# A decoder layer on one core: the shift of the normalized rows moves from an accumulating DMA to an add on GpSimd

## What is computed

```python
    merged = jax.nn.sigmoid(gate_a) * (o_a @ w_branch_a) + jax.nn.sigmoid(gate_b) * (o_g @ w_branch_b)
    x = x + gate1 * (merged @ w_out)
    h2 = rms_norm(x, norm2_g) * (1 + scale2) + shift2
    x = x + gate2 * hier_moe(h2, ...)      # top-2 of 32 experts, each w_gate, w_up (1024 x 512), w_down (512 x 1024)
```

## Time and profile before

| | us |
|---|---|
| median of 3 runs (lowest, highest) | 1292.85 (1291.79, 1295.52) |
| the profiled execution, its own time | 1294.05 |
| its span in the profile | 1292.1 |
| row stage and routing, until the first gather is issued | about 720 to 796 |
| experts | about 802 to 1290 |
| PE busy, DVE busy, ACT busy, POOL busy | 1159.8, 523.0, 224.9, 230.0 |

### The profile page before, as it was taken

The page is one execution under the profiler, slowest core; times in us unless marked ns, Lnnn a source line. Parts: engine busy times, 40 slices in busy tenths (PEclk is TensorE's granted clock), DMA queues, the critical chain, the costliest instruction groups (busy, mean ns, idle before and its releaser), DMA issues.

```text
span 1292.1 us, 20453 instructions
## 1 busy us (share of the span) xinstructions
PE 1159.8 (90%) x7849; PEld 731.6 (57%) x7849; DVE 523.0 (40%) x1094; ACT 224.9 (17%) x506; POOL 230.0 (18%) x279
## 2 busy tenths in 40 slices
PE   4999998999999999999999997999978788778796
PEld 2344443475667668888887455656544354444463
DVE  3398967534253454454454447221211111111112
ACT  4122225331222321101100222000000000000000
POOL 2432344200010411520000001111111101111000
PEclk9999999999999999999999996999999989999999
DMA  9998999998243444224434727999999999999994
GB/s 355 371 287 281 356 378 384 377 386 307 92 142 128 127 118 103 58 64 113 122 131 146 261 65 246 421 416 414 413 420 418 418 415 420 416 414 418 414 414 168
DMA packets 118392, 368.15 MB, mean 285 GB/s; under 512 B 12604, under 2 KB 58573, under 8 KB 98966
## 3 DMA queue, kind: packets, MB, share of 16 engines
q1 hardware_dynamic: 93408, 304.44, 60.8%
q0 software_dynamic: 21328, 55.24, 13.9%
q10 hardware_dynamic: 3558, 7.13, 1.8%
HBM read 354.61 MB, written 22.36 MB: 292 GB/s over the span
## 4 chain that ended last, share of the span: by engine, by line
PE 63%; DMA 24%; SPq 4%; DVE 4%; issue 3%; ACT 2%; ACTq 0%; DVEq 0%; POOLq 0%
PE ps L1941 60%; DMA hx<-in_w_exp_gate 10%; DMA ring<-in_w_exp_gate 6%; DMA ring<-in_w_exp_up 4%; PE ps L1952 3%; SPq L583 2%; DMA ring<-in_cache_v 1%; DMA ring<-in_cache_k 1%; SPq L588 1%; DMA work<-in_x_prompt 1%; DMA h_rows<-ring 1%; SPq L556 1%; DVE work L1896 0%; SPq L554 0%; DVE ring L1316 0%
## 5 line engine op out<-in xcount | busy, mean ns | idle before, releaser
L1941 PE MATMUL ps<-ring,work 128*64 128x256 f32 (+4 forms) x2064 | 294.0, 436 | 42.5 <-DMA ring<-in_w_exp_up 17.0
L1941 PEld LDWEIGHTS ps<-ring,work 128*64 128x64 f32 (+2 forms) x2064 | 156.1, 138 | 162.4 <-issue 83.2
L1941 PE MATMUL ps<-hx,ring 128*128 128x272 f32 x928 | 215.0, 393 | 4.1 <-DVE work L1560 4.1
L1941 PE MATMUL ps<-ring,hx 128*32 128x256 f32 (+3 forms) x1232 | 209.4, 463 | 8.5 <-ACT hx L879 4.2
L1941 PEld LDWEIGHTS ps<-hx,ring 128*128 128x128 f32 x928 | 175.7, 190 | 41.3 <-issue 4.2
L1941 PEld LDWEIGHTS ps<-ring,hx 128*32 128x32 f32 (+1 forms) x1232 | 108.1, 139 | 95.2 <-issue 76.4
L1941 PE MATMUL ps<-work 128*32 128x256 f32 (+12 forms) x1186 | 133.7, 397 | 20.8 <-DVE work L1255 10.0
L1941 PE MATMUL ps<-hx,work 128*64 128x256 f32 (+2 forms) x784 | 113.9, 411 | 22.8 <-DMA hx<-in_w_exp_up 9.0
L1894 DVE TENSOR_TENSOR work<-work,ps 128x256 f32<-128x256 f32 x32 | 13.5, 421 | 251.0 <-ACT work L1200 251.0
L800 POOL DMA_INDIRECT out<-work x32 | 50.5, 1578 | 327.8 <-DVE work L1906 327.8
L1941 PEld LDWEIGHTS ps<-hx,work 128*64 128x64 f32 (+2 forms) x784 | 69.5, 144 | 67.3 <-issue 30.9
(11 more groups left out here) (333 smaller groups left out, 931.0 us busy)
## 6 DMA issues: line engine op xcount, KB each, us to landing
ring<-in_w_exp_gate SPq DMA_DIRECT2D x21, 2048.0 KB, 40.8
ring<-in_w_exp_down SPq DMA_DIRECT2D x42, 1024.0 KB, 39.1
ring<-in_w_exp_up SPq DMA_DIRECT2D x21, 2048.0 KB, 40.4
ring<-in_w_ada SPq DMA_DIRECT2D x12, 2048.0 KB, 17.2
hx<-in_w_exp_gate SPq DMA_DIRECT2D x11, 2048.0 KB, 41.1
hx<-in_w_exp_up SPq DMA_DIRECT2D x10, 2048.0 KB, 38.9
work<-in_w_exp_down SPq DMA_DIRECT2D x20, 1024.0 KB, 39.3
ring<-in_cache_v SPq DMA_DIRECT2D x64, 256.0 KB, 9.6
```

The lines of the kernel that those rows point to most:

```text
L1941: return pe.matmul(out, lhsT, rhs, start=start, stop=stop, **k)
```

## The change

1. **The shift on GpSimd.** ACT's early fill of `h2_dram` is gone. The shift lies in a new tile `row_c` (in slot 5): sample shifts are loaded by ACT beside the other sample rows, the prompt's by SP (`shift_in`) after step 0's store. POOL adds `row_c` in place to each scaled tile, one TENSOR_TENSOR of 128 x 1024 for each step (32 x 1024 for step 0), and counts `h2_full`.
2. **Plain stores.** SP stores each tile to `h2_dram` (`rows_out`), at fixed places in its program: step 0 first, steps 1 and 2 behind the residual stores of steps 2 and 3, step 3 behind the load of expert 2's up, step 4 behind the load of expert 1's gate and the last residual store.
3. **Turned rows in `mergedT`.** `h2T[n]` is now that step's own columns in `mergedT`, five places in place of two, so ACT's copy no longer waits for the router's product (`lg_ps`). `out_part` takes the place of `h2g[1]`.
4. **First gate product.** For expert 0, TensorE starts the gate product on the first half of `xsT` and waits for the second half before k = 4.

```diff
-        h2T = [grid(ring[:, 5, D * (i + 2):D * (i + 3)], KD) for i in range(2)]
-        out_part = grid(ring[:, 5, 3 * D:4 * D], 2)
+        h2T = [mergedT[:, :, TILES[a][0]:TILES[a][0] + TILES[a][1]] for a in LATE]
+        out_part = grid(h2g[1], 2)
+        row_c = ring[:, 5, 2 * D:3 * D]
...
+            def rows_out(n):
+                t0, T = TILES[LATE[n]]
+                sp.wait_ge(s("h2_full"), n + 1)
+                sp.dma_start(h2_dram[t0:t0 + T, :], h2g[n % 2][0:T, :]).then_inc(s(f"h2_out{n % 2}"), 16)
+
+            rows_out(0)
+            sp.dma_start(row_c, bass.AP(tensor=mod_dram.tensor, offset=0, ap=[[0, P], [1, D]])).then_inc(s("shift_in"), 16)
             for n in range(1, PT):
                 residual_out(n)
+                if n > 1:
+                    rows_out(n - 1)
             sp.wait_ge(*stream[BEFORE_EXPERTS[4]][2])
             gate_up_load(2, 1, expert_row(2))
+            rows_out(PT - 1)
             sp.wait_ge(s("out_ps"), 2 * PT + 2)
             gate_up_load(1, 0, expert_row(1))
             residual_out(PT)
+            rows_out(PT)
...
                 pool.wait_ge(s("h2_rows"), n + 1)
-                pool.dma_start(h2_dram[t0:t0 + T, :], h2g[n % 2][0:T, :], accum_op=ALU.add).then_inc(s(f"h2_out{n % 2}"), 16)
+                if n == 0:
+                    pool.wait_ge(s("late_in"), 16 * 3)
+                elif n == 1:
+                    pool.wait_ge(s("shift_in"), 16)
+                v = h2g[n % 2][0:T, :]
+                pool.tensor_tensor(v, v, row_c[0:T, :], ALU.add).then_inc(s("h2_full"), 1)
...
-                if u == 0:
-                    act.wait_ge(s("late_out"), 64)
-                    act.dma_start(h2_dram[0:SEQ, :], late_source(0, 0, [0, SEQ])).then_inc(s("late_in"), 16)
-                    act.dma_start(h2_dram[SEQ:, :], late_source(0, 1, [D, DEC_B], [0, DEC_T])).then_inc(s("late_in"), 16)
...
-            late_rows_in(2, 3, 1, [D, DEC_B], [0, DEC_T])
+            act.wait_ge(s("late_out"), 64)
+            for v, kind in ((row_a, 2), (row_b, 3), (row_c, 0)):
+                act.dma_start(v[0:NS, :], late_source(kind, 1, [D, DEC_B], [0, DEC_T])).then_inc(s("late_in"), 16)
...
-                if n >= 2:
-                    act.wait_ge(s("lg_ps"), n - 1)
-                act.activation(h2T[n % 2][:, 4 * q:4 * q + 4, 0:T], grid(ps[:, 4 + q, 0:4 * T], 4), ACT.Copy).then_inc(s("h2T"), 1)
+                act.activation(h2T[n][:, 4 * q:4 * q + 4, :], grid(ps[:, 4 + q, 0:4 * T], 4), ACT.Copy).then_inc(s("h2T"), 1)
...
-                    dve.wait_ge(s("late_in"), 16 * (4 if n == 0 else 6))
+                    dve.wait_ge(s("late_in"), 16 * (3 if n == 0 else 5))
...
-                pe.wait_ge(s("xsT"), n)
+                ahead = isinstance(e, int) and e == 0
+                pe.wait_ge(s("xsT"), n - 1 if ahead else n)
...
+                        if ahead and m == 0 and k == KD // 2:
+                            pe.wait_ge(s("xsT"), n)
```

More of the change, by code:

```diff
@@ L1109, in _ @@
                 first_taken(OUT_GATE, u)
-                if u == 0:
-                    act.wait_ge(s("late_out"), 64)
-                    act.dma_start(h2_dram[0:SEQ, :], late_source(0, 0, [0, SEQ])).then_inc(s("late_in"), 16)
-                    act.dma_start(h2_dram[SEQ:, :], late_source(0, 1, [D, DEC_B], [0, DEC_T])).then_inc(s("late_in"), 16)
-                elif u == 1:
+                if u == 1:
                     act.wait_ge(s("state_p_out"), 16 * GH)
-                else:
+                elif u > 1:
                     act.wait_ge(s("o_gated"), u - 1)
@@ L1170, in _ @@
                     act.wait_ge(s("h2_gained"), 2)
-                    late_rows_in(2, 3, 0, [0, P])
+                    for v, kind in ((row_a, 2), (row_b, 3)):
+                        act.dma_start(v, late_source(kind, 0, [0, P])).then_inc(s("late_in"), 16)
                 turned_taken(n, 0)
@@ L1907, in dve_step @@
                 dve.tensor_scalar(weighted[par], ps[:, 4 + par, :], weight, None, ALU.mult).then_inc(s("weighted"), 1)
-            dve.wait_ge(s("late_in"), 16 * 16)
+            dve.wait_ge(s("late_in"), 16 * 15)
             for e in range(NE):
@@ L2517, in logits_of @@
                 for k in ks:
-                    last = mm(ps[0:T, 6, m * a:m * a + m], h2T[n % 2][:, k, 0:T], wr[:, k, 0:m], k == 0, k == KD - 1, skip_group_check=True)
+                    last = mm(ps[0:T, 6, m * a:m * a + m], h2T[n][:, k, :], wr[:, k, 0:m], k == 0, k == KD - 1, skip_group_check=True)
                 if ks[-1] == KD - 1:
```

## The result

| us | before | after |
|---|---|---|
| median (lowest, highest), 7 runs each | 1293.37 (1291.79, 1295.52) | 1298.04 (1296.08, 1300.18) |
| the profiled execution, its own time | 1294.05 | 1296.08 |
| its span | 1292.1 | 1294.1 |
| SP issues the residual rows' load: end of the merge, **M** | 707.33 | 705.04 |
| DVE starts the last tile's scaling (step 4, half 1), **S** | 781.23 | 783.61 |

The account below looks back on a forecast made before the run. The expert weight stream bounds the kernel, its start held by the gathers. A gather 0.66 us sooner, less 0.15 for ACT's loads, left 0.5 us; from the 1292.85 median the forecast was 1292.3 us, range 1290.1 to 1294.4.

Parts of the forecast that it names:

- the earlier tiles: Steps 0 to 3, before the last tile: POOL's adds run into DVE, nobody on the path late; without cover, up to 0.5 us a tile.
- What bounds the kernel: Expert phase: the weight stream keeps the DMA engines full, so the end is the stream's start, at 801.87 us, plus a constant.
- The add, the collision, the index: Last tile: POOL's 2.35 us add holds up a DVE add, moving the index 1.68 us to 794.17; forecast case, 62%.
- The plain store: Last tile's row store in SP's queue behind gate load and residual store: lands at 791.5, before the index.
- my case of slow values: Last store: residual lands after 9.8 us as before, at 792.5, and the rows at 793.8 to 795.1; slower-store rival 12%.
- What travels with it: ACT's ten small expert loads move nearer the first gather; cost to the gathers 0 to 0.5 us, taken as 0.15.
- my rivals: Besides the forecast: index not delayed 17%, store late 12%, collisions at steps 1 to 3 reach TensorE 5%, stream not following gathers 4%.
- the tail's terms: Last tile to expert 1's down load: add, store, index, gather 0.66 us sooner, ACT's small loads 0.15; leaves 0.5 us gain.

## Why the prediction was wrong

I forecast 1292.3 us (1290.1 to 1294.4), a gain of 0.5, with 93% on no difference. It became 1298.04, a loss of 4.7 us. The step that failed is the one on the earlier tiles, ahead of the part that I worked out.

- **What bounds the kernel**: right. The stream of weights decides, and its start and the end moved together (2.36 us for down, 2.0 for the span, between the profiles).
- **The add, the collision, the index**: right. The add was forecast at 2.35 us and took it, from S + 4.60 (forecast 4.69). DVE's instruction was stretched to 1.38 us, where I had said 1.8, because it came 1.0 us into the add and not 0.5: the ranking began 0.38 us later, since TensorE's eight small products ahead of it took 1.48 us in place of 1.08, and the add hid that. The index was forecast at 794.17, S + 12.94, and was ready at S + 12.85. The gather was forecast at S + 13.83 and came at 13.81, released by DVE. The Trainium skill (SBUF — State Buffer, "SBUF: two separate sides") says that the two take a shared pair of ports exclusively, for a whole instruction. The trace agrees: 0.16 us became 0.92 to 1.76 in the seven profiles with the add (how much depends on when it comes during it), and stayed 0.16 in the one without.
- **The plain store**: the value was too good. I took 791.5, S + 10.3, on the ground that gate and residual would land after 7.5 us without the accumulate beside them. They took 9.9 and 9.7, about as before, and the store landed near S + 12.4, close to my case of slow values (S + 12.6 and later). Two readings behind it were wrong. The accumulate had not slowed the two loads ahead, and it had not overtaken them: they had landed by 790.7 and 792.5, it landed at 794.83, and POOL's queue moved 0.02 of its 0.5 MB before 790 us. That the error cost nothing is luck: the index was later still, by 0.5 us.
- **What travels with it**: the term was mis-sized. I put the shift of ACT's ten loads at 0.15 us (0 to 0.5); the stretch from gather to down grew by 0.66, and the variant with early loads gives 0.9 back. It took the whole gain of the gather.
- **The earlier tiles**: this is where the sum failed. I looked at the collisions of POOL's adds (they cost nothing: 50.55 us from step 1 to S with and without them) and costed the load of the *prompt's* shift. The load of the *sample* rows' shift, which the same item of the change adds as the third of ACT's small loads, and DVE's wait for all three at step 0 (`late_in` 3), got no term at all. The rows needed were in the trace of before: DVE's step 0 with its idle time ended by TensorE, SP's 6 MB issued just ahead of ACT's loads, and the small loads' last packets at 717, some 2.3 us before they were needed. A third load of the same size behind them had to be asked for its landing. It came 2.99 us after the time at which DVE had begun before.
- **The clock**: no case of mine had TensorE run dry in the row stage and pay for it a second time. The 2.99 us of wait became 4.67.

The range was built from the tail's terms and from the spread of the runs; none of my rivals had a place ahead of step 1, so the one mechanism that decided was outside all of them. The tail came out close to even (0.02 us from S to down), so the sum missed the half microsecond there too, by the ten loads. What isn't settled is the share of the DMA engines that a small load gets beside another queue's megabytes, and why the store of the variant without the last add took 9.6 us.

## What to carry to other kernels

A small load that is added to a group under one semaphore makes every waiter of that group wait for the last of them: give each use its own count, or let only the engine that reads the data wait for it. Price it by what else is queued at that moment in the other queues, not by its bytes, and look at how much time the waiter's present releaser leaves. When an engine that feeds TensorE is made to wait on the path, add to the wait what TensorE's lower clock costs behind it, and ask which reused buffer hands the delay on.

## What the runs showed of the hardware

- A load of 128 KB took 12.05 us behind 6 MB that another queue had just been given, and at most 6.25 when 4 of the 6 were held back. Holding them back moved the loss to ACT's next load, of 1 MB.
- A store issued sooner landed later: S + 4.82 and 9.6 us against S + 6.98 and 5.4 us, in the same queue behind the same 2.5 MB. The gate load ahead of it took 11.9 us in place of 9.9. This is one profile of each.
- TensorE, busy for 0.63 and 0.77 us of two windows of 2 us, fell to a granted clock of 0.50 and kept it for 2 us in which it was fully busy: six products in 4.74 us against 2.84.
- A DVE instruction with two inputs in SBUF waits until POOL's add is over: 1.38 us in place of 0.16, ending 0.03 us behind the add.
